# A hybrid decoder trunk on one core: a weight tile's low part is made between the halves of a job, three jobs ahead

## What is computed

```python
for layer in range(DEPTH):                       # DEPTH = 2
    u = rmsnorm(h, attn_norm[layer])
    (mla_dq, mla_dkv, mla_kr, gla_q, gla_k, gla_v, gla_gd, gla_r,
     hgrn_q, hgrn_f, hgrn_i, hgrn_g, gate_logits) = jnp.split(u @ w_in[layer], offsets, axis=-1)
    o_mla = mla_branch(...)      # softmax attention, 8 heads
    o_gla = gla_branch(...)      # chunked gated linear attention, 4 heads
    o_hgrn = hgrn2_branch(...)   # the same recurrence, gates from a lower bound
    gates = jax.nn.sigmoid(gate_logits).reshape(B, L, N_BRANCH, D_MODEL)
    mixed = (gates[:, :, 0] * (o_mla @ w_mla_o[layer])
             + gates[:, :, 1] * (o_gla @ w_gla_o[layer])
             + gates[:, :, 2] * (o_hgrn @ w_hgrn_o[layer]))
    h = h + mixed @ w_out[layer]
    u = rmsnorm(h, ffn_norm[layer])
    # layer 0: dense SwiGLU, d_ff 2816; layer 1: top 2 of 8 SwiGLU experts, d_expert 3584
```

## Time and profile before

| | |
|---|---|
| median of 3 runs | 1886.82 us (1886.32 to 1887.91) |
| the profiled execution | 1887.6 us, of which the span of instructions is 1885.3 us |
| mean granted TensorE clock | 0.989 |
| busy, share of the span | PE 1817.2 us (96%), DVE 1483.9 us (79%), ACT 1284.4 us (68%), POOL 111.7 us (6%) |
| `lo` instructions of the jobs (L948) | 220, mean 1224 ns |

### The profile page before, as it was taken

How to read it: one execution, slowest core, us unless ns; L and a number is a source line. 1 busy time by engine, 2 the same in 40 slices (tenths; PEclk the granted TensorE clock), 3 DMA queues, 4 the chain that set the end, 5 groups by cost and what they waited for, 6 DMA issues and landing times.

```text
span 1885.3 us, 29527 instructions
## 1 busy us (share of the span) xinstructions
PE 1817.2 (96%) x10740; PEld 1579.3 (84%) x10740; DVE 1483.9 (79%) x1741; ACT 1284.4 (68%) x1632; POOL 111.7 (6%) x95
## 2 busy tenths in 40 slices
PE   7999999899998998999899999999999999999998
PEld 6888888899997888888688888888888888888886
DVE  5868796655547778777698898988989889898897
ACT  5677677443335776775577777777777777777776
POOL 0000002100010000004300100001000010000101
PEclk9999999999999999999899999999999999999999
DMA  5323334455554333335699999999999999999995
GB/s 196 124 90 128 107 102 136 143 171 178 163 176 147 121 105 120 112 108 164 243 406 365 390 381 360 405 367 389 380 360 409 365 389 381 361 406 368 361 407 215
DMA packets 87108, 485.37 MB, mean 257 GB/s; under 512 B 11630, under 2 KB 11934, under 8 KB 43744
## 3 DMA queue, kind: packets, MB, share of 16 engines
q1 hardware_dynamic: 84080, 476.14, 67.4%
q0 software_dynamic: 2944, 8.09, 1.7%
HBM read 477.17 MB, written 8.41 MB: 258 GB/s over the span
## 4 chain that ended last, share of the span: by engine, by line
PE 80%; DVE 10%; ACT 6%; issue 3%; POOL 0%; DMA 0%; POOLq 0%; DVEq 0%; SPq 0%; ACTq 0%
PE bank L1715 11%; PE bank L1716 11%; PE bank L1720 11%; PE bank L1440 8%; PE bank L1442 7%; PE bank L1441 7%; PE bank L1732 5%; PE bank L1733 5%; PE bank L1738 5%; DVE lo L948 2%; ACT hi L666 1%; PE bank L1747 1%; PE bank L1609 1%; PE bank L1589 1%; PE bank L1612 1%
## 5 line engine op out<-in xcount | busy, mean ns | idle before, releaser
L1287 DVE TENSOR_TENSOR mlo<-mraw,mhi 128x2048 fp32r<-128x2048 f32 x281 | 638.7, 2289 | 93.7 <-ACT mhi L879 81.1
L879 ACT ACTIVATE mhi<-mraw 128x2048 fp32r<-128x2048 f32 x283 | 540.5, 1916 | 107.4 <-PE bank L1738 50.5
L1440 PE MATMUL bank<-UH,hi 128*128 128x272 f32 (+1 forms) x1376 | 415.5, 302 | 18.5 <-DVE UL L961 8.6
L1442 PE MATMUL bank<-UH,lo 128*128 128x272 f32 (+1 forms) x1376 | 398.9, 290 | 0.0
L1441 PE MATMUL bank<-UL,hi 128*128 128x272 f32 (+1 forms) x1376 | 397.7, 289 | 0.0
L666 ACT ACTIVATE hi<-raw 128x1024 fp32r<-128x1024 f32 (+1 forms) x220 | 229.3, 1043 | 118.1 <-PE bank L1442 118.0
L1715 PE MATMUL bank<-mhi,xh 128*128 128x512 f32 x768 | 303.7, 395 | 0.0
L948 DVE TENSOR_TENSOR lo<-raw,hi 128x1024 fp32r<-128x1024 f32 (+1 forms) x220 | 266.4, 1224 | 43.0 <-ACT hi L666 42.6
L1716 PE MATMUL bank<-mhi,xl 128*128 128x512 f32 x768 | 299.4, 390 | 0.0
L1440 PEld LDWEIGHTS bank<-UH,hi 128*128 128x128 f32 x1376 | 262.3, 191 | 31.2 <-issue 27.0
L1441 PEld LDWEIGHTS bank<-UL,hi 128*128 128x128 f32 x1376 | 263.3, 191 | 1.1 <-issue 0.5
(11 more groups left out here) (332 smaller groups left out, 2471.3 us busy)
## 6 DMA issues: line engine op xcount, KB each, us to landing
mraw<-in_w_exp SPq DMA_DIRECT2D x336, 1024.0 KB, 5.0
raw<-in_w_dense SPq DMA_DIRECT2D x212, 512.0 KB, 3.3
raw<-in_w_dense SPq DMA_DIRECT2D x8, 384.0 KB, 3.2
wuq<-in_w_uq SPq DMA_DIRECT2D x2, 1024.0 KB, 9.2
mixed<-in_x SPq DMA_DIRECT2D x2, 512.0 KB, 5.1
wukv<-in_w_ukv SPq DMA_DIRECT2D x2, 512.0 KB, 9.2
u_rows<-utok SPq DMA_DIRECT2D x1, 1024.0 KB, 4.1
y_rows<-acc SPq DMA_DIRECT2D x1, 1024.0 KB, 6.1
```

The lines of the kernel that those rows point to most:

```text
L879: A_(mhi[k % MHI][:], mraw[k % MRAW][:], ACT.Copy).then_inc(mhi_made, 1)
L1287: TT(mlo[k % MRAW][:], mraw[k % MRAW][:], mhi[k % MHI][:].bitcast(F32), ALU.subtract).then_inc(mlo_made, 1)
L1440: MM(ps, h, xh_, start=first, stop=False)
L1442: return MM(ps, l, xh_, start=False, stop=last)
```

## The change

`split_lo` no longer stands at the head of a job. It stands between its halves, ahead of `evacuate`, and makes the tile of three jobs ahead, where it was two. The first loop, ahead of job 0, so makes three tiles. Counted in half jobs, DVE comes to a given tile one half earlier.

```diff
-RAW, HI, LOOK, LOOK_LO = 6, 4, 3, 2
+RAW, HI, LOOK, LOOK_LO = 6, 4, 3, 3
...
             for g in range(NG):
-                if g + LOOK_LO < NG:
-                    split_lo(g + LOOK_LO)
                 if g in norm_before:
                     norm(phase, gains[phase], True)
...
                 for half in range(2):
                     if half == 1:
+                        if g + LOOK_LO < NG:
+                            split_lo(g + LOOK_LO)
                         evacuate(g)
                     elif g:
                         finish(g - 1)
```

## The result

The changed kernel takes **1910.28 us** (median of 4 runs, 1908.67 to 1910.88) against 1886.89 us (1886.32 to 1887.91) for the kernel before: 23.4 us more. The ratio is 1.0115, with a 95% interval of 1.0103 to 1.0127. The forecast was 1900.0 us with a range of 1893 to 1908. The direction was right; the size was not, and the time lies 2.3 us outside the range. The profiled execution has a span of 1909.0 us, against 1885.3.

The account below looks back on a forecast made before the run. Mostly PE-bound (80% of the chain), so the change matters only where PE stands still. Layer sums of +4.56 and +4.61 plus 4.0 for both (k) gave +13.2 us: median 1900.0 us, range 1893 to 1908.

Parts of the forecast that it names:

- a rival at 0.17: POOL's additions get no faster (1906.6 us), or another half-clock stretch of PE comes (3.5 us): up to 1910; chance 0.17.
- (b): Tile 18 ahead of the last `KLT` copy (L1193) waits for its `hi`, delaying PE's L1589: +1.56 us, layer 1 +1.74.
- (d): `wo 5` to `wo 7`: `lo` ahead of L1028, tile 40 also ahead of L1203, lengthen PE's waits: +1.84 and +2.09 us.
- (i): `wo 8`: L1028 must wait for tile 62, whose `hi` ends late: +1.09 us, layer 1 +1.25.
- (k): `wo 0` to `wo 3`: `lo` in series, POOL relieved, period 3.86 to 4.15 us: +1.8, layer 1 +2.2.
- (a): Where DVE stands 0.49 us before clearing `S`, the tile can fill the gap: -0.25 us per layer.
- (c): `r 2` to `v 4`: one `lo` leaves the chain ending at PE's L1540: -1.13 us, layer 1 -1.1.
- The `evacuate` that comes later at 240 us: Layer 0's `f`, `q` and `v`: `evacuate` comes 1.14 us later, absorbed by a 1.15 us stall behind ACT: 0.
- (g): Tile 54 at 271.23 us lengthens PE's wait at 271.37: +1.14 us; layer 1 only +0.3, as PE is slow there.
- The rival of no change: The moved `lo` runs while DVE waits for PE's half anyway, so PE covers it: 1887 us; chance 0.05.
- The rival of a faster kernel: The longer lead readies every `lo` and fills DVE's gaps, gaining at most 4.9 us: 1882 us; chance 0.04.
- partly absorbed terms: Half of (b), (d), (g) and (i) is taken back by the next stall: 1892 to 1896 us; chance 0.14.

Follow-up runs that it names:

- cover_after: The changed kernel with spare matrix products on PE ahead of sixteen of its waits in the mixers; 1905.67 us (ratio 1.0092).
- before_again: The kernel before, unchanged, profiled once more; 1888.32 us.
- place: The changed kernel with the `lo` still ahead of `evacuate` but made for two jobs ahead, not three; 1896.78 us (ratio 1.0051).
- only_c: The kernel before with only tiles 24 to 36 of each mixer (`r 0` to `v 5`) in the new place; 1888.67 us (ratio 0.9994).
- after_again: The changed kernel, unaltered, profiled once more; 1910.84 us.
- only_d: The kernel before with only tiles 38, 39 and 40 of each mixer (`wo 5` to `wo 7`) in the new place; 1895.07 us (ratio 1.0038).
- only_k: The kernel before with only tiles 67 to 70 of each mixer (`wo 0` to `wo 3`) in the new place; 1891.15 us (ratio 1.0022).
- closure: The changed kernel with 17 tiles of each mixer, at all places read as costly, put back to the old place; 1885.19 us (ratio 0.9986).
- only_b: The kernel before with only tile 18 of each mixer (ahead of the last `KLT` copy) in the new place; 1892.09 us (ratio 1.0025).
- all_but_bd: The changed kernel with tiles 18, 38, 39 and 40 of each mixer put back to the old place; 1899.83 us (ratio 1.0064).

## Why the prediction was wrong

**The step that failed** is the treatment of the clock. The sum took the granted clock of the trace before as given, and left its change to a rival at 0.17. Against that rival it said: "the new stalls are 1 to 3 us apiece, and only one place of two layers shows such a fall". It priced that rival at one stretch, 3.5 us. The runs showed six stretches in the mixers, worth 11.9 us in the ledger, where there had been one. cover_after showed that PE's standing still brings them. Without them the mixers are 8.3 us shorter, net of the spare products and of the waits for DVE that come out from under the half clock; about 1.5 of these are the stretch that the kernel before has too. So the clock's share of the 23.4 us is some 7 to 12 us, no more exactly. That rival's upper end, 1910, is the measured time, but by luck: it was made of 6.6 us for a POOL without relief, which did not come, and of one stretch.

The signs were in the trace before. "Only one place" holds for the mixers alone: at the norms, where PE waits 2.8 to 2.9 us (22.9, 363.5 and 572.9 us), stretches stand as well. A wait of PE of 1.58 us stood right ahead of the stretch in the earlier trace rows:

```profile
809.61 0.37 PE L1589 MATMUL bank<-V,KLT 16*128 16x128 f32 x1 [1.58 <-DVE KLT L1193]
```

And the mixers held four waits of that length or more; by my own terms (b), (d), (i) and (k) there had to be more of them, and the trace after has eight, of 1.57 to 2.5 us. That three of the four before had no stretch behind them (one was of 2.06 us) misled me; before_again shows one of these with a stretch.

**The queue's part, point by point** (layer 0, layer 1, by the ledger):

- (a), forecast -0.25 each: 0 in both. The wait of `gate 9` goes and the chain behind it swallows that, as forecast.
- (b), forecast +1.56 and +1.74: +1.65 and +1.81. The reading of ACT's `hi` was right, and place shows that it is the wait and not the `lo` that costs.
- (c), forecast -1.13 and -1.1: the step at L1540 is there, -1.06 and -1.12, but 0.7 us is lost ahead of it, at the first products of `r` jobs (150.1, 154.1 and 158.0 us before), where tiles 28 to 30 now stand ahead of L1019. Net some -0.4 each, and the same in only_c's ledger. The term was oversized.
- (d), forecast +1.84 and +2.09: +1.2 and +1.1 beside the clock's 3.0 and 3.1, which hide the rest. Without a stretch it is +1.9 in layer 0 of after_again and +2.5 in both layers of only_d.
- The `evacuate` that comes later at 240 us, forecast 0: +1.13, then -1.07 at the stall that absorbs it. Right.
- (g), forecast +1.14 and +0.3: +1.14 in layer 0. In layer 1 it was hidden under the half clock, as forecast, and comes out as part of +1.93 in cover_after.
- A term that the sum does not have: tile 53 ahead of L1193 in the HGRN2 branch, +0.85 and +0.93. PE waits 2.12 us there now, where it waited 1.27.
- (i), forecast +1.09 and +1.25: +1.14 and +1.32.
- (k), forecast +1.8 and +2.2: +1.7 and, without the clock's part, about +1.0; +1.7 in both layers of cover_after. only_k alone gives +3.8 us beside the 4.0 forecast. The period of 4.00 against 4.15 says that the relief of POOL is full, and a little larger than I took it. The exclusive lock that the Trainium skill describes (SBUF — State Buffer, "SBUF: two separate sides") agrees with this: two additions take 1.50 us with no `lo` beside them, 2.49 with one.
- The SwiGLU, `wout` and the expert layer, forecast 0: closure, which keeps the SwiGLU's tiles in the new place, is not slower than the kernel before.

The rival of no change fell with the result, and only_d alone is 7.8 us slower. The rival of a faster kernel fell at the point named for it: at `wo 7` the `lo` doesn't end before PE's half does, and the wait grew from 1.74 to 2.07. That of partly absorbed terms had (d) right in this trace, where the half clock hides near half of it, but not the sum. That the queue's 13.1 us meet the 13.2 forecast is partly luck: (d) and (k) came out some 3 us smaller, and the missed term, (c) and (a) some 3.7 us larger.

## What to carry to other kernels

An instruction that is put ahead of the one that frees a bank costs its own time only if that one is late already, but it costs everything that it has to wait for itself: ask when its input is made, not how long it takes. Where a change lengthens waits of PE, give the clock a term of its own, a stretch of PE at 1.2 GHz behind the wait, and read in the trace before which waits already have such a stretch behind them. The two prices don't add in full, because behind a stretch a wait on another engine can shrink; and whether a stretch comes is uncertain, so the term widens the range. Before spending effort on the clock, look at who sets the pace there: spare products raised the mean clock from 0.989 to 0.996 and moved the time by nothing where DVE or the spare products themselves were the bound. And one trace's clock is one sample: stretches come and go between executions of the same kernel.

## What the runs showed of the hardware

- PE's granted clock fell to 0.50 behind waits of 1.57 to 2.5 us in the mixers, and not behind all of them: the wait of 1.58 in layer 0 of only_b had no stretch behind it, that of 1.75 in layer 1 had. It fell behind shorter ones too, of 1.29 us at 261 us in before_again and of 1.25 at 211 us in all_but_bd. Two traces of one kernel differ in which falls occur (262 and 740 us).
- Products that nobody reads kept PE's clock up: with PE busy 2.00 of 2 us in each window shown around the waits, the clock stayed at 1.00 (cover_after).
- Two POOL additions of 128x272 beside a DVE subtraction of 128x1024 took 2.49 us, and 1.50 without; the subtraction took 1.67 beside them and 1.22 without.
- With the same work, PE's busy time was 1817.2 us in one order and 1828.6 in another. With more of the span at half clock the same work counts as more busy time.
